# Attention by transposes of the bare exponentials: the one over the sums multiplies the values' sums instead of the probabilities

## The chip, the cores and the metric

The kernel runs on one NeuronCore of a Trainium2 chip. The metric is the device time of one execution in microseconds (us). Engines are named as in the profile: PE is TensorE's matmul side and PEld its weight load, DVE is VectorE, ACT is ScalarE, POOL is GpSimd, SP is SyncE.

## The reference

A model of 256 tokens of width 1024 runs through one hybrid block (a dilated attention of three groups of eight heads beside a state-space branch, then a gated feed-forward), and then, beside 256 context tokens, through four more layers: gated linear attention, a convolution, a full attention, gated linear attention again, each with a feed-forward. Everything is fp32. The change touches only the two softmax attentions:

```python
# hybrid block: 8 heads x 3 dilation groups, 256 queries, width 64 per head
logits = q @ k.T * HEAD_DIM ** -0.5 + bias          # causal, masked
p = exp(logits - m); o = (p @ v) / sum(p)           # for each group, then
attn = sum over the 3 groups of alpha * o           # alpha = softmax of the groups' log sums
# layer 2 of the second model: 16 query heads, 4 key heads, 512 tokens (256 + 256 context)
o = softmax(q @ k.T * ATTN_SCALE) @ v               # context queries see only the context's keys
```

The alpha-weighted sum over groups is the same as one softmax over the keys of all three groups, and the kernel computes it so: one maximum and one sum per head and query.

## The kernel before

The residual x lies in SBUF with features on the partitions. The weights stream in as 282 blocks of 1 MB through four raw buffers (SP issues the loads); ACT rounds each block to its high half (`split`, L1099), DVE makes the low half (L1716), and PE multiplies by three products, high-high, high-low and low-high (`three`, L493 to L498). No engine is scheduled by a planner: each engine's program is written out in order, and semaphores that count up join them. What stands in front of a waiting instruction on its engine goes first, always.

**The first attention** (hybrid block) runs beside eight blocks of the z projection. `PAIRS` (L376) are eight steps n: head pair j of 0 to 3, query tile qt of 0 and 1. A step has 6 key tiles of 128 when qt is 0 (3 groups, 2 heads, 1 tile) and 12 when qt is 1.
- PE, for each n (main loop of `products`): the scores of step n + 1 (L651), 3 parts of the z projection, the values of step n - 1 (`values`, L667), 2 parts, `turn(n)` (L672 to L683), 3 parts. A part is 6 matmuls of 256 columns. `turn` makes groups of up to four 128x128 tiles in banks 0 and 1 in turns; the third group of a qt = 1 step waits until DVE has taken the first. A turned tile is a matmul of the probabilities' tile (stationary) by a diagonal matrix that holds one over the sum of each query.
- ACT, for each n: the split of a z block, two exponentials with their sums (L1205), a copy of a z column, then after `recip_ready` two diagonals, identity times one over the sum (L1212), another z copy.
- DVE, for each n: after the exponentials the reciprocal (L1864), `front(n + 1)` (scores plus bias, maxima, L1842 to L1852), the split of a z block, the copies of the turned groups to SBUF (L1875), and after every second step `pair` (L1857), which copies 128x256 of values for the output projection. ACT and POOL then make its halves.
- After the loop PE goes on with four blocks of the output projection of this branch. They wait for a counter that DVE raises behind the last `pair` (L1885).

**The second attention** (layer 2) has nothing beside it. `PAIR_STEPS` (L446) are 32 steps n: head pair j of 0 to 7, query tiles in the order 0, 2, 1, 3. Tiles 0 and 1 see 512 keys, 2 and 3 see 256, so even n are wide (4 key tiles for each of the 2 heads) and odd n narrow (2 for each).
- PE, for each n: scores of n + 2 (L1001, after the exponentials of n have left its banks), `turn(n)` (L1013; by diagonals, one bank for each head), `values(n - 1)` (L1026; the two heads in the two column halves of the array). Turned banks 4 and 5, value banks 2 and 3.
- ACT, for each n: two exponentials with sums (L1541), then after the reciprocal two diagonals (L1550).
- DVE, for each n: maxima of n + 1 (L2392, L2396), copies of the turned tiles of n - 1 (L2409, one for each head), the reciprocal (L2402), and every fourth step a copy of 128x512 of values (`pair`, L2415).
- Four blocks of the output projection follow on PE (L496 to L498).

Of the kernel before, what the change touches and what calls it, by code (L numbers as in the profile page):

```python
# [132 lines left out]
class Role:  # L133
# [41 lines left out]
    "diag_ready", "head_squares", "heads_summed", "qstat_read", "qn_ready", "rot_ready", "rot_taken"])  # L175
# [111 lines left out]
def place(nc, ctx):  # L287
# [75 lines left out]
    with ExitStack() as st:  # L363
# [5 lines left out]
        b.diag = [[sb(st, f"diag{i}{j}", [P, P]) for j in range(2)] for i in range(2)]  # L369
# [16 lines left out]
def diagonal_of(b, n, odd):  # L386
    o = P * (2 * (n % 2) + odd)
    return b.sg[0][:, o:o + P]
# [58 lines left out]
SCORE_BANKS, TURNED_BANKS, VALUE_BANKS = ((0, 1), (6, 7)), (4, 5), (2, 3)  # L447

# [35 lines left out]
def products(nc, b, R, pe, ring):  # L484
# [187 lines left out]
    def turn(n):  # L672

        j, qt = PAIRS[n]
        for group in turned_groups(qt):
# [3 lines left out]
            for i, (odd, gr, kt) in enumerate(group):  # L679
                pe.wait_ge(R.sems["diag_ready"], 2 * n + odd + 1)  # L680
                last = mm(bank[m % 2][:, i * P:(i + 1) * P], b.logits[n % 2][:, odd, gr, kt * P:(kt + 1) * P],
                          diagonal_of(b, n, odd), start=True, stop=True)
            last.then_inc(*R.made("turned_ready"))  # L683

# [3 lines left out]
    for n in range(len(PAIRS)):  # L688
# [3 lines left out]
        if n:  # L692
            values(n - 1)
        go_on(parts, 2)
# [3 lines left out]
    values(len(PAIRS) - 1)  # L698
    R.next("turned_taken", R.value("m turned_ready"))
    R.next("diag_ready", 2 * len(PAIRS))  # L700
# [267 lines left out]
    def attention():  # L968
# [36 lines left out]
        def turn(n):  # L1005

            tiles = 4 if PAIR_STEPS[n][1] < 2 else 2
            for odd in range(2):
                pe.wait_ge(*R.next("diag_ready"))
                if n:  # L1010
                    pe.wait_ge(*R.next("turned_taken"))
                for i in range(tiles):
                    last = mm(bank[TURNED_BANKS[odd]][:, i * P:(i + 1) * P],  # L1013
                              b.prob[n % 2][odd][:, i * P:(i + 1) * P], b.diag[n % 2][odd][:], start=True, stop=True)
                last.then_inc(*R.made("turned_ready"))

        def values(n):
            j, qt = PAIR_STEPS[n]
            tiles = range(4) if qt < 2 else range(2, 4)
            pe.wait_ge(R.sems["turned_taken"], turned_before + 2 * (n + 1))  # L1020
            if n % 4 == 0 and j >= 2:
                pe.wait_ge(R.sems["part_lo"], parts_before + j - 1)
            for i, kt in enumerate(tiles):
                for odd in range(2):
                    base = HD * odd
                    last = mm(bank[VALUE_BANKS[j % 2]][base:base + HD, qt * P:(qt + 1) * P],  # L1026
                              b.av[:, kt, (j // 2) * HD:(j // 2 + 1) * HD], b.pt[n % 2][odd][:, i, :],
# [15 lines left out]
        R.next("exp_ready", 2 * GROUP_HEADS)  # L1043
# [6 lines left out]
        R.next("turned_taken", 2)  # L1050
        R.next("exp_ready", 4)
# [29 lines left out]
def splits_and_functions(nc, b, R, act, ring):  # L1081
# [114 lines left out]

    tables()
# [487 lines left out]
def vectors(nc, b, R, dve, ring):  # L1685
# [175 lines left out]
    for n, (j, qt) in enumerate(PAIRS):  # L1861
# [7 lines left out]
        if n:  # L1869
            dve.wait_ge(R.sems["values_ready"], 2 * n)  # L1870
# [752 lines left out]
```

## Time and profile before

| | us |
|---|---|
| three runs | 3223.01, 3230.93, 3230.63 (median 3230.63) |
| the profiled execution | 3230.28 |
| its span | 3228.5 |
| PE busy in it | 3042.9 (94%) |
| DVE, ACT, POOL busy | 1579.1 (49%), 1234.1 (38%), 302.0 (9%) |
| first attention, about | from 157 to 245 of the span |
| second attention, about | from 2220 to 2328 of the span |

The profile is one execution, taken by the hardware profiler. Lines are those of the kernel before. In a timeline the columns are the start in us from the span's start, the time in us, engine, line, operation, what it writes and reads, the shape, the number of instructions merged into the row, and in brackets the idle time before it and what ended it. An fp32 matmul is issued as two MATMUL records, a transpose as one. Ends of matmuls are modelled, so that one row overlaps the next: distances between starts are the better measure.

### The profile page before, as it was taken

The page shows a single profiled execution, that of the slowest core. Times are in us where ns is not written, and L with a number is a line of the kernel's source. Part 1 is how long each engine was busy: PE and PEld are TensorE (multiplying, and loading weights), DVE is VectorE, ACT ScalarE, POOL GpSimd, SP SyncE. Part 2 cuts the span into 40 slices and gives each one's busy share as a digit, 9 for nine tenths or more (in the row PEclk, how much of TensorE's full clock was granted, in tenths as well). Part 3 has the DMA queues.
Part 4 walks back from the last instruction along what each step waited for, and adds up shares of the span by engine and source line. Part 5 has one row for each costly group of instructions (what it writes and reads, how often), then busy time and mean ns, then how long its engine had stood idle before and what let it go on. Part 6 is the DMA issues. An engine that isn't in the chain of part 4 may idle for free.

```text
span 3228.5 us, 45698 instructions
## 1 busy us (share of the span) xinstructions
PE 3042.9 (94%) x19734; PEld 2493.5 (77%) x19734; DVE 1579.1 (49%) x2204; ACT 1234.1 (38%) x1756; POOL 302.0 (9%) x288
## 2 busy tenths in 40 slices
PE   8999888997998999999989999999999999897999
PEld 7898878996864778886657788876777888684799
DVE  4467756554456433333864333346643333446554
ACT  3245564445234422224344222344542223425443
POOL 1000001101001101111001001200010111000111
PEclk9999999998999999999999999999999999998899
DMA  7836314454210444224115432240044322221253
GB/s 281 305 114 233 131 53 170 165 180 179 93 52 27 158 168 152 97 92 144 66 40 192 162 130 93 103 148 27 14 169 170 138 97 92 80 79 37 108 183 131
DMA packets 59609, 407.66 MB, mean 126 GB/s; under 512 B 6504, under 2 KB 9832, under 8 KB 11024
## 3 DMA queue, kind: packets, MB, share of 16 engines
q1 hardware_dynamic: 58368, 401.02, 34.6%
q0 software_dynamic: 1040, 3.71, 0.4%
q8 instruction: 156, 2.56, 0.3%
q14 instruction: 45, 0.37, 0.0%
HBM read 403.62 MB, written 1.09 MB: 125 GB/s over the span
## 4 chain that ended last, share of the span: by engine, by line
PE 85%; DVE 7%; ACT 6%; issue 2%; POOL 1%; DMA 0%; DVEq 0%; ACTq 0%; POOLq 0%
PE bank L496 24%; PE bank L497 23%; PE bank L498 23%; PE bank L563 3%; DVE wlo L1716 2%; ACT whi L1099 2%; PE bank L932 1%; PE bank L572 1%; ACT part L1359 1%; PE bank L884 1%; PE bank L878 1%; PE bank L1013 1%; PE bank L888 1%; DVE small L2392 1%; ACT xnhi L1362 1%
## 5 line engine op out<-in xcount | busy, mean ns | idle before, releaser
L1716 DVE TENSOR_TENSOR wlo<-raw,whi 128x2048 fp32r<-128x2048 f32 x282 | 646.3, 2292 | 434.6 <-ACT whi L1099 434.2
L1099 ACT CAST whi<-raw 128x2048 fp32r<-128x2048 f32 x282 | 536.6, 1903 | 586.3 <-PE bank L498 586.2
L496 PE MATMUL bank<-xnhi,whi 128*128 128x512 f32 (+1 forms) x1776 | 681.5, 384 | 39.0 <-DVE xnlo L2101 14.3
L497 PE MATMUL bank<-xnlo,whi 128*128 128x512 f32 (+1 forms) x1776 | 664.6, 374 | 0.0
L498 PE MATMUL bank<-xnhi,wlo 128*128 128x512 f32 (+1 forms) x1776 | 662.4, 373 | 0.0
L496 PEld LDWEIGHTS bank<-xnhi,whi 128*128 128x128 f32 x1776 | 344.2, 194 | 140.7 <-issue 46.4
L498 PEld LDWEIGHTS bank<-xnhi,wlo 128*128 128x128 f32 x1776 | 344.7, 194 | 58.0
L497 PEld LDWEIGHTS bank<-xnlo,whi 128*128 128x128 f32 x1776 | 345.4, 194 | 53.0 <-issue 0.2
L496 PE MATMUL bank<-hidhi,whi 128*128 128x512 f32 (+1 forms) x1024 | 373.4, 365 | 0.2 <-DVE wlo L1716 0.2
L497 PE MATMUL bank<-hidlo,whi 128*128 128x512 f32 (+1 forms) x1024 | 371.6, 363 | 0.0
L498 PE MATMUL bank<-hidhi,wlo 128*128 128x512 f32 (+1 forms) x1024 | 371.3, 363 | 0.0
L496 PE MATMUL bank<-xn1hi,whi 128*128 128x256 f32 x992 | 295.8, 298 | 11.7 <-POOL xn1lo L1605 8.9
L497 PE MATMUL bank<-xn1lo,whi 128*128 128x256 f32 x992 | 285.0, 287 | 0.0
L498 PE MATMUL bank<-xn1hi,wlo 128*128 128x256 f32 x992 | 284.7, 287 | 0.0
L2120 DVE SCALAR_TENSOR_TENSOR x<-bank,mod,x 128x256 f32<-128x256 f32 x264 | 117.1, 479 | 328.5 <-PE bank L498 328.5
L1605 POOL TENSOR_TENSOR hidlo<-part,hidhi 128x512 fp32r<-128x512 f32 (+1 forms) x128 | 145.5, 1157 | 1079.4 <-ACT hidhi L1109 1079.4
L1587 ACT ACTIVATE sg<-bank 128x512 f32<-128x512 f32 (+1 forms) x128 | 69.6, 544 | 395.0 <-PE bank L498 395.0
L496 PEld LDWEIGHTS bank<-hidhi,whi 128*128 128x128 f32 x1024 | 193.2, 189 | 35.1 <-issue 4.9
L2452 DVE SCALAR_TENSOR_TENSOR part<-bank,sg 128x512 f32<-128x512 f32 (+1 forms) x128 | 79.9, 624 | 283.2 <-ACT sg L1587 262.2
L498 PEld LDWEIGHTS bank<-hidhi,wlo 128*128 128x128 f32 x1024 | 193.3, 189 | 30.3
L497 PEld LDWEIGHTS bank<-hidlo,whi 128*128 128x128 f32 x1024 | 193.3, 189 | 29.5
L496 PEld LDWEIGHTS bank<-xn1hi,whi 128*128 128x128 f32 x992 | 194.3, 196 | 26.6 <-issue 13.9
(317 smaller groups left out, 4301.7 us busy)
## 6 DMA issues: line engine op xcount, KB each, us to landing
raw<-in_wall SPq DMA_DIRECT2D x378, 1024.0 KB, 4.8
x<-in_x SPq DMA_DIRECT2D x2, 1024.0 KB, 7.3
bias<-relative_offsets POOLq DMA_DIRECT2D x2, 768.0 KB, 7.0
x<-relative_offsets POOLq DMA_DIRECT2D x2, 768.0 KB, 9.4
out<-x SPq DMA_DIRECT2D x1, 1024.0 KB, 4.8
vec<-in_vec SPq DMA_DIRECT2D x1, 665.0 KB, 9.7
cst<-in_cst SPq DMA_DIRECT2D x1, 465.0 KB, 10.3
rope<-in_rope POOLq DMA_DIRECT2D x1, 320.0 KB, 3.4
```

Source lines behind the costliest of these rows:

```text
L496: mm(out, wh, xh, start=first, stop=False)
L497: mm(out, wh, xl, start=False, stop=False)
L498: return mm(out, wl, xh, start=False, stop=last)
L563: last = mm(bank_of_sums[strip:strip + 32, 0:UC], b.cond[:, kk, :], w[:, kk, :], start=(kk < 4), stop=(kk >= 4))
L572: last = mm(bank_of_sums[:, o:o + 2], b.modrow[:, c * P:(c + 1) * P], cst("strips"), start=True, stop=True)
L878: last = mm(out[d], b.att[h % 2][d][half[d]:half[d] + 64, n[d] // 2, :], vv[d], start=(s % 4 == 0), stop=False)
L1099: nc.scalar.copy(b.whi[u % SPL][:], b.raw[pos % RAW][:]).then_inc(*R.made("hi_ready"))
L1587: fn(b.sg[c][:, 0:t], bank_of(c)[:, 0:t], ACT.Relu).then_inc(*R.made("gate_ready"))
L1605: tt(lo, src, hi, ALU.subtract).then_inc(*R.made("part_lo"))
L1716: ttn(b.wlo[u % SPL][:], b.raw[blocks[u] % RAW][:], b.whi[u % SPL][:], ALU.subtract).then_inc(*R.made("lo_ready"))
L2120: last = stt(b.x[:, ch, o:o + S], bank_of(c)[:, o:o + S], mcol(i, v, ch, s), b.x[:, ch, o:o + S], ALU.mult, ALU.add)
L2452: stt(part(t), bank_of(c)[:, 0:t], 0.0, b.sg[c][:, 0:t], ALU.max, ALU.mult) \
```

## The change

Both attentions turn the bare exponentials, by PE's transpose instead of a matmul by a diagonal. ACT makes no diagonals. One over the sums is made once for each head pair (second attention) or still each step but later in DVE's order (first), and PE spreads it in rows: `spread_inverses` multiplies each column of inverses, repeated 64 times as the stationary operand, by the identity, into a free half bank (first attention, 4 matmuls for each head pair) or bank 5 (second, 8 matmuls for each head pair). ACT copies that to SBUF (`copy_normaliser`), and `pair` on DVE multiplies the values' sums by it where it copied them. In the second attention the narrow steps turn both heads into one bank, so that DVE takes them with one copy of 512 columns instead of two of 256. New waits: transposes wait for the exponentials alone; ACT's exponentials of n wait until n - 2 is turned. The list of semaphores and the buffers `diag` change to match.

```diff
@@ -383,9 +382,15 @@
-def diagonal_of(b, n, odd):
-    o = P * (2 * (n % 2) + odd)
-    return b.sg[0][:, o:o + P]
+def inverses_of(b, j, first, tiles):
+    o = first + 2 * tiles * (j % 2)
+    return b.small[:, o:o + 2 * tiles].rearrange("p (q o) -> p q o", o=2)
+def turns_of_first():
+    return sum(len(turned_groups(qt)) for _, qt in PAIRS)
@@ -445,6 +450,25 @@
 SCORE_BANKS, TURNED_BANKS, VALUE_BANKS = ((0, 1), (6, 7)), (4, 5), (2, 3)
+def turns_by(n):
+    return 3 * ((n + 1) // 2) + 2 * ((n + 1) % 2)
+def turned_exps(b, n, odd):
+    return b.pt[0][odd][:, :, :] if n % 2 == 0 else b.pt[1][0][:, 2 * odd:2 * odd + 2, :]
+def normaliser_of(b):
+    return b.pt[1][1][:].rearrange("p a t -> p (a t)")
+def sums_of(b, j):
+    o = 48 * (j % 2)
+    return b.small[:, o:o + 8].rearrange("p (q o) -> p q o", o=2)
@@ -677,10 +701,22 @@
             for i, (odd, gr, kt) in enumerate(group):
-                pe.wait_ge(R.sems["diag_ready"], 2 * n + odd + 1)
-                last = mm(bank[m % 2][:, i * P:(i + 1) * P], b.logits[n % 2][:, odd, gr, kt * P:(kt + 1) * P],
-                          diagonal_of(b, n, odd), start=True, stop=True)
+                pe.wait_ge(R.sems["exp_ready"], 2 * n + odd + 1)
+                last = nc.tensor.transpose(bank[m % 2][:, i * P:(i + 1) * P],
+                                           b.logits[n % 2][:, odd, gr, kt * P:(kt + 1) * P], ident)
             last.then_inc(*R.made("turned_ready"))
+    def spread_inverses(out, inverses):
+        for qt in range(inverses.shape[1]):
+            for odd in range(2):
+                last = mm(out[odd * HD:(odd + 1) * HD, qt * P:(qt + 1) * P],
+                          inverses[:, qt, odd:odd + 1].to_broadcast([P, HD]), ident, start=True, stop=True)
+        last.then_inc(*R.made("norm_ready"))
+    def normaliser(j):
+        pe.wait_ge(R.sems["recip_ready"], 2 * j + 2)
+        spread_inverses(bank[5][:, S:T2], inverses_of(b, j, 32, 2))
@@ -691,13 +727,16 @@
             values(n - 1)
+            if n % 2 == 0:
+                normaliser(n // 2 - 1)
         go_on(parts, 2)
...
     values(len(PAIRS) - 1)
+    normaliser(GROUP_HEADS // 2 - 1)
     R.next("turned_taken", R.value("m turned_ready"))
-    R.next("diag_ready", 2 * len(PAIRS))
+    R.next("recip_ready", len(PAIRS))
     stage(4, b.ao, S, kc=4, fresh=True)
@@ -1005,26 +1044,35 @@
         def turn(n):
             tiles = 4 if PAIR_STEPS[n][1] < 2 else 2
+            if n:
+                pe.wait_ge(R.sems["turned_taken"], turned_before + turns_by(n - 1) - (tiles == 2))
             for odd in range(2):
-                pe.wait_ge(*R.next("diag_ready"))
-                if n:
-                    pe.wait_ge(*R.next("turned_taken"))
+                pe.wait_ge(R.sems["exp_ready"], exps_before + 2 * n + odd + 1)
+                if odd and n and n % 4 == 0:
+                    pe.wait_ge(R.sems["norm_copied"], norms_before + n // 4)
+                out = bank[TURNED_BANKS[odd if tiles == 4 else 0]]
+                o = odd * S if tiles == 2 else 0
                 for i in range(tiles):
-                    last = mm(bank[TURNED_BANKS[odd]][:, i * P:(i + 1) * P],
-                              b.prob[n % 2][odd][:, i * P:(i + 1) * P], b.diag[n % 2][odd][:], start=True, stop=True)
-                last.then_inc(*R.made("turned_ready"))
+                    last = nc.tensor.transpose(out[:, o + i * P:o + (i + 1) * P],
+                                               b.prob[n % 2][odd][:, i * P:(i + 1) * P], ident)
+                if odd or tiles == 4:
+                    last.then_inc(*R.made("turned_ready"))
+        def normaliser(j):
+            pe.wait_ge(R.sems["recip_ready"], recips_before + j + 1)
+            spread_inverses(bank[TURNED_BANKS[1]], inverses_of(b, j, 32, 4))
         def values(n):
...
             tiles = range(4) if qt < 2 else range(2, 4)
-            pe.wait_ge(R.sems["turned_taken"], turned_before + 2 * (n + 1))
+            pe.wait_ge(R.sems["turned_taken"], turned_before + turns_by(n))
             if n % 4 == 0 and j >= 2:
...
                     last = mm(bank[VALUE_BANKS[j % 2]][base:base + HD, qt * P:(qt + 1) * P],
-                              b.av[:, kt, (j // 2) * HD:(j // 2 + 1) * HD], b.pt[n % 2][odd][:, i, :],
+                              b.av[:, kt, (j // 2) * HD:(j // 2 + 1) * HD], turned_exps(b, n, odd)[:, i, :],
                               start=(i == 0), stop=(i == len(tiles) - 1))
@@ -1040,15 +1088,16 @@
         turned_before, parts_before = R.value("w turned_taken"), R.value("w part_lo")
-        R.next("exp_ready", 2 * GROUP_HEADS)
+        recips_before, norms_before = R.value("w recip_ready"), GROUP_HEADS // 2
+        exps_before = R.next("exp_ready", 2 * GROUP_HEADS)[1]
         for n in range(len(PAIR_STEPS)):
...
                 values(n - 1)
-        R.next("turned_taken", 2)
-        R.next("exp_ready", 4)
+            if n % 4 == 3:
+                normaliser(n // 4)
         values(len(PAIR_STEPS) - 1)
@@ -1194,6 +1243,10 @@
+    def copy_normaliser():
+        act.wait_ge(*R.next("norm_ready"))
+        nc.scalar.copy(b.sg[0][:, 0:S], bank[5][:, S:T2]).then_inc(*R.made("norm_copied"))
     tables()
@@ -1202,19 +1255,17 @@
             L = b.logits[n % 2][:, odd, :, 0:nk]
-            fn(L, L, ACT.Exp, bias=b.small[:, 20 + col:21 + col], accum_out=b.small[:, 24 + col:25 + col]) \
+            fn(L, L, ACT.Exp, bias=b.small[:, 20 + col:21 + col],
+               accum_out=b.small[:, 24 + col:25 + col]) \
                 .then_inc(*R.made("exp_ready"))
         z_column(0)
-        act.wait_ge(*R.next("recip_ready"))
-        o = CST["ident"][0]
-        for odd in range(2):
-            col = 28 + 2 * (n % 2) + odd
-            fn(diagonal_of(b, n, odd), b.cst[:, o:o + P], ACT.Copy, scale=b.small[:, col:col + 1]) \
-                .then_inc(*R.made("diag_ready"))
+        if n and qt == 0:
+            copy_normaliser()
         z_column(1)
...
             part(b.ao[0][:, n // 2 - 1, :], width=S)
+    copy_normaliser()
     part(b.ao[0][:, 3, :], width=S)
@@ -1534,21 +1585,20 @@
         def exponent(n):
-            nk = T2 if PAIR_STEPS[n][1] < 2 else S
+            j, qt = PAIR_STEPS[n]
+            nk = T2 if qt < 2 else S
             act.wait_ge(*R.next("neg_max"))
+            if n >= 2:
+                act.wait_ge(R.sems["turned_ready"], turns_of_first() + turns_by(n - 2))
             for odd in range(2):
...
                    bias=b.small[:, 20 + col:21 + col], scale=HD ** -0.5,
-                   accum_out=b.small[:, 24 + col:25 + col]).then_inc(*R.made("exp_ready"))
-        def diagonal(n):
-            act.wait_ge(*R.next("recip_ready"))
-            o = CST["ident"][0]
-            for odd in range(2):
-                col = 28 + 2 * (n % 2) + odd
-                fn(b.diag[n % 2][odd][:], b.cst[:, o:o + P], ACT.Copy, scale=b.small[:, col:col + 1]) \
-                    .then_inc(*R.made("diag_ready"))
+                   accum_out=sums_of(b, j)[:, qt, odd:odd + 1]).then_inc(*R.made("exp_ready"))
+        def copy_normaliser():
+            act.wait_ge(*R.next("norm_ready"))
+            nc.scalar.copy(normaliser_of(b), bank[TURNED_BANKS[1]][:]).then_inc(*R.made("norm_copied"))
@@ -1556,9 +1606,11 @@
             exponent(n)
-            diagonal(n)
+            if n and n % 4 == 0:
+                copy_normaliser()
             if n >= 5 and n % 4 == 1:
                 part(b.xn[0][:, n // 4 - 1, :], width=T2)
+        copy_normaliser()
         part(b.xn[0][:, KC - 1, :], width=T2)
@@ -1853,19 +1905,22 @@
     def pair(c):
         dve.wait_ge(R.sems["values_ready"], 4 * (c + 1))
-        cp(part(S).rearrange("p (a t) -> p a t", t=P),
-           bank[5][:, 0:S].rearrange("p (a t) -> p a t", t=P)[:, :, ::-1]).then_inc(*R.made("part_ready"))
+        dve.wait_ge(*R.next("norm_copied"))
+        way = lambda a: a.rearrange("p (a t) -> p a t", t=P)[:, :, ::-1]
+        ttn(part(S).rearrange("p (a t) -> p a t", t=P), way(bank[5][:, 0:S]), way(b.sg[0][:, 0:S]), ALU.mult) \
+            .then_inc(*R.made("part_ready"))
...
         col = 2 * (n % 2)
-        dve.wait_ge(*R.next("exp_ready", 2))
-        nc.vector.reciprocal(b.small[:, 28 + col:30 + col], b.small[:, 24 + col:26 + col]) \
-            .then_inc(*R.made("recip_ready"))
         if n + 1 < len(PAIRS):
...
         split()
+        dve.wait_ge(*R.next("exp_ready", 2))
+        nc.vector.reciprocal(inverses_of(b, j, 32, 2)[:, qt, :], b.small[:, 24 + col:26 + col]) \
+            .then_inc(*R.made("recip_ready"))
         if n:
@@ -2396,23 +2451,21 @@
-        def inverse(n):
-            col = 2 * (n % 2)
-            dve.wait_ge(*R.next("exp_ready", 2))
-            nc.vector.reciprocal(b.small[:, 28 + col:30 + col], b.small[:, 24 + col:26 + col]) \
-                .then_inc(*R.made("recip_ready"))
+        def inverse(j):
+            dve.wait_ge(*R.next("exp_ready", 8))
+            nc.vector.reciprocal(inverses_of(b, j, 32, 4), sums_of(b, j)).then_inc(*R.made("recip_ready"))
         def take_turned(n):
             nt = 4 if PAIR_STEPS[n][1] < 2 else 2
-            for odd in range(2):
+            for odd in range(2 if nt == 4 else 1):
                 dve.wait_ge(*R.next("turned_ready"))
-                cp(b.pt[n % 2][odd][:, 0:nt, :],
-                   bank[TURNED_BANKS[odd]][:, 0:nt * P].rearrange("p (a t) -> p a t", t=P)) \
+                cp(b.pt[n % 2][odd][:, :, :], bank[TURNED_BANKS[odd]][:].rearrange("p (a t) -> p a t", t=P)) \
                     .then_inc(*R.made("turned_taken"))
         def pair(j):
             dve.wait_ge(*R.next("values_ready", 4))
-            cp(part(T2), bank[VALUE_BANKS[j % 2]][:]).then_inc(*R.made("part_ready"))
+            dve.wait_ge(*R.next("norm_copied"))
+            ttn(part(T2), bank[VALUE_BANKS[j % 2]][:], normaliser_of(b), ALU.mult).then_inc(*R.made("part_ready"))
@@ -2422,13 +2475,12 @@
         for n in range(len(PAIR_STEPS)):
-            if n == 0:
-                inverse(0)
             if n + 1 < len(PAIR_STEPS):
...
                 take_turned(n - 1)
-                inverse(n)
+            if n % 4 == 3:
+                inverse(n // 4)
             if n >= 5 and n % 4 == 1:
```

## Rows read from the trace of the kernel before

**Rows 1.** The page, part 4: the chain that ended last, by engine.
```profile
PE 85%; DVE 7%; ACT 6%; issue 2%; POOL 1%; DMA 0%; DVEq 0%; ACTq 0%; POOLq 0%
```

**Rows 2.** Windows: length, busy us by engine, granted clock, DMA share, GB/s; the two attentions.
```profile
160.00:250.00 90.00, 85.67 (x768) 79.15 (x768) 56.62 (x88) 39.75 (x77) 4.60 (x6) 1.00 0.34 112
2232.00:2320.00 88.00, 86.43 (x750) 62.81 (x750) 63.74 (x169) 51.50 (x166) 7.65 (x6) 1.00 0.01 1
```

**Rows 3.** Timeline of PE, one round of two steps in the second attention.
```profile
2235.89 1.13 PE L1001 MATMUL bank<-aqk 64*128 64x512 f32 x4
2236.95 2.05 PE L1013 MATMUL bank<-diag,prob 128*128 128x128 f32 x16
2238.93 0.66 PE L1026 MATMUL bank<-pt,av 128*64 128x128 f32 x8
2239.51 0.70 PE L1001 MATMUL bank<-aqk 64*128 64x256 f32 x4
2240.33 1.16 PE L1013 MATMUL bank<-diag,prob 128*128 128x128 f32 x8
2241.42 1.09 PE L1026 MATMUL bank<-pt,av 128*64 128x128 f32 x16
2242.48 1.13 PE L1001 MATMUL bank<-aqk 64*128 64x512 f32 x4
```

**Rows 4.** Timeline of DVE and ACT in that round.
```profile
2237.09 1.29 DVE L2392 TENSOR_REDUCE small<-bank 128x1 f32<-128x512 f32 x2 [1.54 <-PE bank L1001]
2238.49 1.28 DVE L2409 COPY pt<-bank 128x512 f32<-128x512 f32 x2
2239.76 0.67 DVE L2415 COPY part<-bank 128x512 f32<-128x512 f32 x1
2240.35 0.74 DVE L2392 TENSOR_REDUCE small<-bank 128x1 f32<-128x256 f32 x2
...
2240.99 0.68 ACT L1541 ACTIVATE prob<-bank,small 128x512 f32<-128x512 f32 x1
```

**Rows 5.** Groups of PE by line and shape: records, busy us, mean ns.
```profile
L1013 PE MATMUL bank<-diag,prob 128*128 128x128 f32 x384 | 52.4, 287 | 3.5 <-ACT diag L1550 2.0
L713 PE MATMUL bank<-cst,xs 128*128 128x128 f32 x32 | 4.8, 276 | 2.8 <-DVE dt L1926 1.6 <-DVE xdt L1940 1.1
```

**Rows 6.** Timeline of PE: four transposes in the linear attention, and what follows.
```profile
881.36 0.60 PE L827 MATMUL bank<-cst,part 128*128 128x128 f32 x4
881.88 0.69 PE L832 MATMUL bank<-qb,part 128*64 128x64 f32 x16
```

**Rows 7.** Timeline of PE in the first attention: turned tiles and what follows them.
```profile
165.10 1.50 PE L681 MATMUL bank<-sg,logits 128*128 128x128 f32 x12
...
175.76 3.07 PE L681 MATMUL bank<-sg,logits 128*128 128x128 f32 x24
178.59 0.36 PE L496 MATMUL bank<-xn1hi,whi 128*128 128x256 f32 x1
...
221.44 1.16 PE L681 MATMUL bank<-sg,logits 128*128 128x128 f32 x8 [0.81 <-DVE turned L1875]
```

**Rows 8.** Timeline at the end of the first attention.
```profile
243.45 1.53 PE L667 MATMUL bank<-turned,v 128*64 128x128 f32 x24
245.05 0.42 DVE L1857 COPY part<-bank 128x256 f32<-128x256 f32 x1 [1.66 <-PE bank L667]
...
245.63 0.36 PE L496 MATMUL bank<-aohi,whi 128*128 128x256 f32 x1 [0.66 <-issue]
```

**Rows 9.** Timeline of PE: first and last wide step turned in the second attention.
```profile
2222.86 3.07 PE L1013 MATMUL bank<-diag,prob 128*128 128x128 f32 x16
...
2322.04 2.05 PE L1013 MATMUL bank<-diag,prob 128*128 128x128 f32 x16 [0.60 <-ACT diag L1550]
```

**Rows 10.** Windows, columns as in rows 2: linear attention's end; modulation rows before it.
```profile
1031.00:1040.00 9.00, 9.00 (x62) 3.79 (x60) 6.79 (x16) 2.48 (x8) 2.50 (x2) 1.00 0.00 0
788.00:798.00 10.00, 8.37 (x61) 4.34 (x60) 5.16 (x10) 5.97 (x12) 0.00 (x0) 0.50 0.85 308
```

More of the change, by code:

```diff
@@ L174 @@
     "dw_based", "dw_ready", "mean_summed", "mean_ready", "mean_taken", "centred", "ln_ready",
-    "diag_ready", "head_squares", "heads_summed", "qstat_read", "qn_ready", "rot_ready", "rot_taken"])
+    "norm_ready", "norm_copied", "head_squares", "heads_summed", "qstat_read", "qn_ready", "rot_ready", "rot_taken"])
 def unit_plan():
@@ L368, in place @@
         b.pt = [[sb(st, f"pt{i}{j}", [P, 4, P]) for j in range(2)] for i in range(2)]
-        b.diag = [[sb(st, f"diag{i}{j}", [P, P]) for j in range(2)] for i in range(2)]
     b.bank = [ctx.enter_context(nc.psum_tensor(f"bank{i}", [P, 512], F32)) for i in range(8)]
```

## The prediction

> **What bounds the kernel now.** The chain that ended last comes first: PE holds 85% of it and no DMA is in it [rows 1], so a stage shortens only if PE's own time or PE's waits in it shrink. Then the windows of the two attentions [rows 2]. In both PE is busy nearly throughout (85.7 of 90 us and 86.4 of 88 us) at the full granted clock; DVE has 72% of the second, ACT 59%, the DMA engines almost nothing. So both attentions are PE's, and the reader should see that the two engines that lose work here, ACT and a little of DVE, are not what bounds.
>
> The timeline of one round of the second attention (a wide step and a narrow one) says what PE does with its time [rows 3]. From start to start: wide scores 1.06, wide turning 1.98, narrow values 0.58, narrow scores 0.82, narrow turning 1.09, wide values 1.06; the next round begins 6.59 us after this one. Turning is 3.07 of it, 47%. The narrow scores themselves need about 0.62 (0.70 busy less an overlap of 0.08, as elsewhere in these rows), so 0.20 a round is a wait, for a diagonal. The first round is slower, and the last wide turning waited 0.60 for its diagonal [rows 9].
>
> **The change, part by part.**
>
> *Turning.* An fp32 matmul leaves two records, a transpose one: 192 matmuls of the second attention are 384 records, the 32 transposes of the state-space part are 32 [rows 5]. Eight records more cost 1.98 - 1.09 = 0.89, 0.111 each [rows 3]. Four transposes took 0.52 to the next line's start, 0.11 or so each plus a remainder [rows 6]. So one 128x128 tile falls from 0.22 to 0.11. The bounds of the price: 0.11 below, and 0.15 above, the 4.8 us over 32 of the state-space part [rows 5], which holds the tails of short bursts; I take the lower with a remainder of 0.12 a burst. Wide turning becomes 1.00 (between 8 x 0.11 + 0.08 and the 1.09 of eight matmul records), narrow 0.56 (0.52 to 0.64). That saves 0.98 + 0.53 = 1.51 a round.
>
> *Normaliser on PE, second attention.* Eight matmuls for each head pair, 64 columns wide, the two heads in alternate halves of the array: the shape of the wide values, sixteen records, 1.06 [rows 3]. It could be no less; at worst 2 x 1.06 if stationary operands that are one column repeated load slowly. I take 1.06, or 0.53 a round. The inverse that it waits for is made on DVE right behind the copy that the values before it wait for, so it should find it ready.
>
> *A round afterwards.* 1.06 + 1.00 + 0.58 + 0.62 + 0.56 + 1.06 + 0.53 = 5.41. Now what is late next. DVE finished the maxima and began the first copy 2.60 after the round's start and the second 0.64 later [rows 4]; it still does so, for the maxima depend on the scores alone. The narrow turning would start at 3.26 (1.06 + 1.00 + 0.58 + 0.62) and needs the first copy, at 3.24 and a handing-over of 0.06; the wide values would start at 3.85 and need the second, at 3.94. That is 0.1 of wait. So 5.5 a round against 6.57 (13.15 for four steps), and 1.07 saved. DVE's own sum: 1.40 maxima, 1.20 copies, 0.85 narrow maxima [rows 4], 0.64 for one 512-column copy instead of two of 256, half of a pair's 0.6, that is 4.4 to 4.7 of 5.5: it fits, with little to spare. ACT loses 1.4 of diagonals a round and gets a copy of 512 columns each second one, about as long as an exponential's 0.68 [rows 4]. That copy stands behind the exponentials of step 4k and ahead of those of 4k + 1, and waits for PE's normaliser, whose results are there some 0.2 us into the round of step 4k. Copy to 0.9, two narrow exponentials at 0.5 to 0.7 each to 2.3 at the latest; the narrow scores that need their banks start at 2.64: covered by at least 0.3. Without the cover each microsecond late costs one, eight times. The wait on the turning of n - 2 lies a round back and is met. `pair` as a product reads one operand more; I cost it like the copy, 0.67 [rows 4], and up to twice that, which would make DVE late in four-step turns by at most 0.6 x 8.
>
> *Second attention, sum.* Fifteen ordinary rounds 16.0. In the first round the wide turning took 3.07 at a clock that was mostly half, against 2.05 later [rows 9]; with half the records 1.5 goes, and 0.4 of waits. In the last, the 0.60 for the diagonal goes. Together 18.5. The last normaliser stands ahead of the last values, so the `pair` behind them is not later; the output projection reaches its last eighth some 5 us after it starts anyway.
>
> *First attention.* PE has z parts to do between, but it is the bound all the same, so less turning is time. Turning 12 tiles took 2.83 to the next line [rows 7]; 6 tiles half of that less a wait, 1.3. Two of the four turnings of 12 had to wait longer for DVE (0.81 in one [rows 7]); about 18 us in all for eight steps. Afterwards 6 x 0.11 = 0.66, and for 12 tiles the third group must wait for the first to be copied: 0.60 (four transposes to their end [rows 6]), 0.06, a copy of 0.69, 0.06, then 0.44: 1.85. Four of each: 10.0, if DVE is on time. It should be: the reciprocal moves behind `front(n + 1)` and the split on DVE, so these two no longer wait for the exponentials, and nothing on PE but the normaliser waits for the reciprocal. This saves 7.9. Three normalisers in the loop, 8 records like narrow values, 0.58 each, take 1.7. The fourth stands in an open chain: values end, DVE copies at 245.05, PE goes on at 245.63 [rows 8]; now a normaliser 0.58, ACT's copy (0.4, at most 0.68) and handings lie between, 1.1. Net 5.1. No DMA is issued elsewhere; SP's loads are released by the splits and by nothing else here.
>
> *Total.* 23.6 off the profiled execution's 3230.3, which lies 0.4 under the median: **3206.7**, so 3207. The runs before lie 8 apart; a difference under 0.3% (10 us) is what a measurement of this kernel can't tell from none.
>
> **A rule that speaks against it.** In the linear attention's end PE did nothing but matmuls on a half or a quarter of the array and a few transposes, and the granted clock was 1.00 for 9 us; in the modulation rows, PE busy 8.4 of 10 us with matmuls 32 columns wide, it was 0.50 throughout [rows 10]. [...] After the change only half-array matmuls and transposes are left in the second attention, the full-array matmuls are gone. The Trainium skill, page "TensorE: Matmul & The Clock Gate", section "Part 4: PE-mode transpose", says that transposes don't count as busy for the clock and the full rate does not engage for them; by this page alone the stage would lean on the scores, values and normalisers, and might run at half clock, 3241 to 3275 by the sums of the third rival below instead of 3207. No row here shows a stretch of transposes alone.
>
> **The rivals.**
> 1. *Forecast*, chance 0.75: 3207.
> 2. *DVE's copies are late*, 0.13: with one set of turned banks, PE waits in every round for a copy, by one copy's length (0.64). For it: DVE at 80% of the round and a margin of 0.0 to 0.1. Against it: DVE starts the maxima as soon as the scores are there. 16 x 0.64 = 10: 3217. With both copies late, 3227, which is no change.
> 3. *The clock falls in the second attention*, 0.06, slower. PE's 5.41 a round becomes 5.41 x 1.8 = 9.7 (the factor between the 1.5 of the first, partly slow turning [rows 9] and the 2 of the two levels, nearer to 2 because that turning ended at full clock). All the stage: +3.1 x 16 = +50, 3275 with the 5 of the first attention off. Half of the time, which I take as the case: +16 x (7.6 - 6.57) = +16, less 5 in the first attention, 3241. It decides from about a third of the stage. Against it: the 9 us at 1.00 of half-array work [rows 10].
> 4. *A transpose costs as much as the matmul here*, 0.02: only waits go (3.2 + 0.6 + some 1), and normalisers stay (8.5 + 1.7 + 1.1): 3230 + 6.5 = 3237. The single records of rows 5 and 6 speak against it.
> The rest, 0.04, is a small gain under 10 us from several of these.
>
> **How the numbers follow.** The forecast's own range: the tile's price (0.11 to 0.13 over 264 tiles, +5), the runs' spread of 8 and 2 of clock phases elsewhere: 3199 to 3212. With the second rival the range is 3199 to 3217. Slower by over 0.3%: 0.08 (3 and 4); within 0.3%: 0.07 (the worse end of 2, and the rest); faster: 0.85.
>
> **What would show it.** In the profile after: turned tiles as 192 and 72 single records at distances of 0.11; rounds of 5.5 in the second attention, no PE wait on ACT in them, waits on DVE's copies under 0.2 each; the wide values of a round 1.06; the stage from first scores to output projection 18 to 19 us shorter; clock 1.00 from the second round on. In the first attention the third group of each qt = 1 step waits about 0.5 for DVE, and the gap ahead of the output projection grows by 1. A stage at clock 0.5, rounds over 6, or ACT held by `norm_ready` past the scores of the next step would make it wrong.

## The result and the profile after

The kernel after takes 3210.48 us (median of four runs, 3206.19 to 3212.88), the kernel before beside it 3226.82 (four runs, 3222.85 to 3230.93). The ratio is 0.9946, 95% interval 0.9933 to 0.9959: 16.3 us or 0.5% faster. The forecast was 3207, with a range of 3199 to 3217. So the total fell into the range, but partly for wrong reasons. One of the two attentions gave 0.6 us more than forecast, and the other 7.8 us less.

The profiled execution took 3206.19 us with a span of 3204.4 (before 3228.5). The chain that ended last, by engine:

```profile
PE 86%; DVE 6%; ACT 5%; issue 1%; POOL 1%; DMA 0%; DVEq 0%; ACTq 0%; POOLq 0%
```

It is PE's as before [rows 1]. Each attention is measured from its first scores to the first matmul of its output projection. For the second attention of the kernel before, that is from 2208.02 to 2327.93 of the span, so it starts some 12 us before the "about 2220" given above:

| us | before | after | change | forecast |
|---|---|---|---|---|
| first attention | 88.27 | 82.58 | -5.7 | -5.1 |
| second attention | 119.90 | 109.24 | -10.7 | -18.5 |
| from the first attention's end to the second's start | 1962.39 | 1955.07 | -7.3 | 0 |
| whole span | 3228.5 | 3204.4 | -24.1 | -23.6 |

The two attentions together give 16.4, close to the 16.3 of the medians. The 7.3 between them lie in code that the change does not touch; the experiments show below that they come and go without it. The span's 24.1 against the forecast's 23.6 is therefore an accident.

Windows of the kernel after, with the columns of rows 2: the first attention, the start of the second, and its rest.

```profile
160.00:235.00 75.00, 72.59 (x662) 66.47 (x662) 52.50 (x82) 32.11 (x59) 3.13 (x4) 1.00 0.37 125
2204.00:2212.00 8.00, 6.11 (x23) 3.37 (x23) 5.73 (x14) 1.64 (x6) 0.00 (x0) 0.57 0.01 3
2212.00:2300.00 88.00, 78.01 (x754) 51.79 (x752) 63.21 (x145) 41.70 (x131) 8.76 (x7) 1.00 0.00 1
```

In the second attention PE is busy 78.0 of 88 us, where before it was 86.4 of 88 [rows 2]: a tenth of the stage has become idle. The granted clock is 1.00 throughout. So the clock does not explain the missing gain; PE waits. For what, the waits of PE in this stage say (in total, how often, the longest):

```profile
PE bank L1040 <- ACT prob L1595: 9.0, 6, 1.5
PE bank L1024 <- DVE aqk L2414: 3.8, 1, 3.8
PE bank L1040 <- DVE aqk L2422: 1.9, 1, 1.9
PE bank L1056 <- DVE pt L2462: 1.0, 1, 1.0
```

The first line is new: six times 1.5 us for ScalarE's exponentials. The two lines below it stand in the kernel before too, at its lines 985 and 1001. The last is one wait at the end of the stage, where the kernel before waited for diagonals. The timeline of PE over four steps shows the place:

```profile
2219.39 1.13 PE L1040 MATMUL bank<-aqk 64*128 64x512 f32 x4
2220.45 1.10 PE L1056 MATMUL bank<-cst,prob 128*128 128x128 f32 x8
...
2223.32 1.09 PE L1074 MATMUL bank<-pt,av 128*64 128x128 f32 x16
2225.92 1.13 PE L1040 MATMUL bank<-aqk 64*128 64x512 f32 x4 [1.50 <-ACT prob L1595]
2226.98 1.09 PE L1056 MATMUL bank<-cst,prob 128*128 128x128 f32 x8
2228.01 0.66 PE L1074 MATMUL bank<-pt,av 128*64 128x128 f32 x8
2228.59 0.70 PE L1040 MATMUL bank<-aqk 64*128 64x256 f32 x4
2229.26 0.66 PE L1056 MATMUL bank<-cst,prob 128*128 128x128 f32 x4
2229.86 1.09 PE L1074 MATMUL bank<-pt,av 128*64 128x128 f32 x16
2230.78 1.04 PE L713 MATMUL bank<-cst,small 128*64 128x128 f32 x16
2231.76 1.13 PE L1040 MATMUL bank<-aqk 64*128 64x512 f32 x4
```

The rounds alternate: 6.53 from 2219.39 to 2225.92 with the wait, 5.84 from there to 2231.76 without. Before, they took 6.56 and 6.59 in turns ([rows 3] show a 6.59). Turned tiles are single records as forecast: wide turning takes 1.03 to the next start, narrow 0.60, the normaliser 0.98. What ScalarE waited for stands in its timeline and DVE's in the late round:

```profile
2220.59 1.29 DVE L2447 TENSOR_REDUCE small<-bank 128x1 f32<-128x512 f32 x2 [1.63 <-PE bank L1040]
2221.91 0.17 DVE L2451 TENSOR_SCALAR small<-small 128x2 f32<-128x2 f32 x1
2221.99 1.28 DVE L2462 COPY pt<-bank 128x512 f32<-128x512 f32 x2
2223.19 0.68 DVE L2468 TENSOR_TENSOR part<-bank,pt 128x512 f32<-128x512 f32 x1
...
2223.90 0.62 ACT L1158 CAST xnhi<-part 128x512 fp32r<-128x512 f32 x1 [2.89 <-DVE part L2468]
2224.43 0.68 ACT L1595 ACTIVATE prob<-bank,small 128x512 f32<-128x512 f32 x1
```

The maxima of step 4k + 2 are known at 2222.08. Its exponentials start at 2224.43, 2.35 later, though ScalarE was idle for 2.89. Ahead of them in ScalarE's order stands a cast of the head pair's values (`part`, issued where n is 4k + 1). It waits for DVE's product, which stands behind the two copies. Everything in this chain (maxima, copies, product, cast, two exponentials, PE's scores that need their bank) was there before the change. PE simply used to be slower than it. From start to start, the rows give scores 1.20, maxima 1.40, copies 1.20, product 0.71, cast 0.53 and exponentials 1.49, which is 6.53 in all.

In the first attention the change did what was forecast. PE's timeline, a step with 12 tiles, and the end:

```profile
175.06 1.04 PE L705 MATMUL bank<-cst,logits 128*128 128x128 f32 x8
176.51 0.66 PE L705 MATMUL bank<-cst,logits 128*128 128x128 f32 x4 [0.41 <-DVE turned L1930]
176.92 0.36 PE L520 MATMUL bank<-xn1hi,whi 128*128 128x256 f32 x1
...
236.86 1.53 PE L691 MATMUL bank<-turned,v 128*64 128x128 f32 x24
238.22 0.61 PE L713 MATMUL bank<-cst,small 128*64 128x128 f32 x8
238.87 0.37 ACT L1248 COPY sg<-bank 128x256 f32<-128x256 f32 x1 [1.37 <-PE bank L713]
239.33 0.42 DVE L1912 TENSOR_TENSOR part<-bank,sg 128x256 f32<-128x256 f32 x1 [2.53 <-ACT sg L1248]
...
239.92 0.36 PE L520 MATMUL bank<-aohi,whi 128*128 128x256 f32 x1 [1.09 <-issue]
```

Twelve tiles take 1.86 to the next line (before 2.83 [rows 7]). From the last values to the output projection it is 3.06 instead of 2.18 [rows 8].

### The profile page after: what moved, and what is told of

The parts are those of the page before. It is cut to its first block, busy times and chain, and to the rows that moved or that the text cites. A ratio compares the mean times of both kernels' runs of the same rounds, so it can differ in the third digit from the quotient of the medians.

```text
span 3204.4 us, 45388 instructions
## 1 busy us (share of the span) xinstructions
PE 3015.1 (94%) x19630; PEld 2464.6 (77%) x19630; DVE 1573.4 (49%) x2164; ACT 1215.1 (38%) x1688; POOL 301.8 (9%) x288
## 3 DMA queue, kind: packets, MB, share of 16 engines
HBM read 403.62 MB, written 1.09 MB: 126 GB/s over the span
## 4 chain that ended last, share of the span: by engine, by line
PE 86%; DVE 6%; ACT 5%; issue 1%; POOL 1%; DMA 0%; DVEq 0%; ACTq 0%; POOLq 0%
PE bank L520 25%; PE bank L521 24%; PE bank L522 23%; PE bank L587 3%; DVE wlo L1768 2%; ACT whi L1148 1%; PE bank L596 1%; PE bank L971 1%; PE bank L923 1%; ACT part L1410 1%; PE bank L917 1%; PE bank L1040 1%; PE bank L927 1%; PE bank L1056 0%; ACT xnhi L1413 0%
```

## The experiments

Eight kernels were run, four of them more than once (experiments 1, 2, 4 and 5); the other times are single executions. "Two steps" and "four steps" are distances between the starts of scores in the first and the second attention; "stage" is as in the table above. The kernel before ran on the same chips (medians 3224.08 and 3224.12).

**1. The cast later.** The suspected wait alone is taken out of its place; the work stays.

```diff
@@ ScalarE, loop over the second attention's steps n
-            if n >= 5 and n % 4 == 1:
+            if n >= 6 and n % 4 == 2:
                 part(b.xn[0][:, n // 4 - 1, :], width=T2)
```

> The changed kernel with one edit: in the second attention ACT rounds the pair's values (the cast that waits for the multiplication by the normaliser) behind the exponentials of step 4k + 2 instead of ahead of them. In the changed kernel PE waits 1.50 us for ACT once in four steps, and four steps take 12.37. Theory A (the cast waits for DVE's pair and holds the exponentials of 4k + 2, whose maxima are ready 2.3 us earlier): the wait goes, four steps take 10.9 to 11.0, the stage from its first scores to the output projection 99 to 101 us instead of 109.3, and the kernel is about 9 us faster than the changed one, near 0.992 of the one before. Rival B (DVE's order, copies and pair ahead of the maxima, is what is late): the wait stays at 1.0 or more, four steps over 12, no more than 2 us gained.

Measured: 3197.72 us (3196.89 to 3198.67), ratio to before 0.9916 (0.9901 to 0.993). Its interval lies wholly under that of the kernel after. The stage is 100.22, 9.0 shorter, which is the six waits of 1.50. Four steps are 4.96 + 5.84 = 10.80. DVE and ACT around the cast, and the window of the stage:

```profile
2224.58 0.17 DVE L2451 TENSOR_SCALAR small<-small 128x2 f32<-128x2 f32 x1
2224.65 1.28 DVE L2462 COPY pt<-bank 128x512 f32<-128x512 f32 x2
2224.78 0.69 ACT L1595 ACTIVATE prob<-bank,small 128x512 f32<-128x512 f32 x1 [1.10 <-DVE small L2451]
2225.85 0.68 DVE L2468 TENSOR_TENSOR part<-bank,pt 128x512 f32<-128x512 f32 x1
...
2226.57 0.62 ACT L1158 CAST xnhi<-part 128x512 fp32r<-128x512 f32 x1 [0.34 <-DVE part L2468]
```
```profile
2212.00:2295.00 83.00, 82.04 (x782) 55.08 (x780) 67.12 (x152) 45.22 (x137) 8.88 (x7) 0.99 0.01 1
```

The exponentials now start with their maxima's end, and what ends ScalarE's idle time is DVE's small tile, not `part`. PE is busy 82.0 of 83 us. That settles the cause of the missing time, and this kernel beats both others.

**2. The product ahead of the copies.** It shortens the same chain at another link and leaves the cast where it was.

```diff
@@ DVE, loop over the second attention's steps n
+            if n >= 5 and n % 4 == 1:
+                pair(n // 4 - 1)
             if n:
                 take_turned(n - 1)
             if n % 4 == 3:
                 inverse(n // 4)
-            if n >= 5 and n % 4 == 1:
-                pair(n // 4 - 1)
```

> The kernel after with one move on VectorE: the product of the head pair is issued ahead of the two copies of the turned exponentials of step 4k+1's round, not behind them. ScalarE's cast stays between the exponentials of 4k+1 and 4k+2. Theory A (ScalarE's queue is held at that cast until the product lands): the cast can start about 1.28 us earlier (the two copies that stood ahead of the product), so the exponentials of 4k+2 are no longer late by 1.5 us but by 0.2 or so; in exchange the copies stand 0.68 later, and TensorE's values of 4k wait some 0.3 to 0.7 for them. Four steps come to 11.2 to 11.7 us, the stage to 102 to 106 us, the kernel 4 to 7 us under the kernel after. Theory B (VectorE's whole work in that round is too long and ScalarE's order does not matter): the same work stands in the round, so four steps stay at 12.4 and the stage at 109.

Measured: 3201.45 us (3199.41 to 3201.81), ratio 0.9923 (0.9906 to 0.9939). Four steps are 5.75 + 5.83 = 11.58, the stage 104.64. The waits of PE in the stage:

```profile
PE bank L1056 <- DVE pt L2462: 5.7, 8, 0.8
PE bank L1024 <- DVE aqk L2414: 3.8, 1, 3.8
```

The wait for the exponentials is gone, though DVE's work is the same, so theory B falls. In its place PE waits up to 0.8 for the copies, which now stand behind the product. This is the second rival of the prediction, made real: DVE's order has no room for 0.68 us ahead of the copies.

The kernel gained more than the 4 to 7 us that were expected: 9.0 from median to median, or 6.3 if each is taken against the kernel before in its own comparison (22.7 against 16.3). The stage explains 4.6 of it; the rest was not traced.

**3. The cast later in the kernel before.**

> The kernel before with the cast of the pair's values moved on ScalarE behind the exponentials of 4k+2, as in the first experiment. Theory A (the wait exists only because the change made TensorE's round shorter than the chain product, cast, exponentials): in the kernel before the chain was covered, so the second attention stays at 119 to 120 us, four steps at 13.1. Theory B (the cast's place costs the same in both kernels and the change only inherits it): the stage shortens by 6 to 9 us here too, to 111 to 113.

Measured: the stage 118.59 (before 119.90), rounds 6.55 and 6.56, one run of 3222.70. Theory A. Before the change the queue cost at most 0.03 a round. It became a cost only as PE's own round fell under 6.53.

**4. and 5. One attention at a time.** The first of these kernels has the change in the first attention alone, the other in the second alone.

> Only the first attention changed, the second as before. Theory: by the two traces the first attention's end came 5.7 us earlier, so this one is 5 to 7 us faster than the kernel before (ratio about 0.998), with two steps in 20.05 us instead of 22.06. Rival (the other 7 us that the changed kernel's trace gains between 300 and 800 us belong to the change, not to the phase of the clock): 10 to 13 us faster.

> Only the second attention changed, the first as before. Theory: its stage takes 109.3 us as in the changed kernel instead of 119.9, the kernel is 10 to 11 us faster than before (ratio about 0.9967), the gains of the two halves add up. Rival (part of the gain of the second attention needs the first's): stage above 111 us.

Measured: first alone 3217.85 us (3216.26 to 3227.18), ratio 0.9982 (0.9972 to 0.9992); second alone 3213.09 us (3211.18 to 3219.77), ratio 0.9971 (0.9961 to 0.9982). Two steps of the first are 20.03 where it is changed, 21.70 to 22.07 where not (the later ones; the earliest pairs are shorter in both). The second's stage is 109.24 where it is changed, 119.33 where not. The gains of 6.2 and 11.0 us add up to 17.2, against 16.3 for both. So the rival of 10 to 13 us for the first alone falls, and no effect of one part on the other is visible beyond the spread of the runs. The trace of the first attention alone has a stage of 84.12 and that of the second alone, whose first attention is the old one, 89.15. Both began at a lower granted clock (0.79 from 157 to 165), and there the gain is 5.0; at full clock from the start it is the 5.7 of the table.

**6. Matmuls by the identity instead of transposes.** The new order of the work stays, the cheaper operation goes.

```diff
@@ both turnings (that of the second attention is shown)
-                    last = nc.tensor.transpose(out[:, o + i * P:o + (i + 1) * P],
-                                               b.prob[n % 2][odd][:, i * P:(i + 1) * P], ident)
+                    last = mm(out[:, o + i * P:o + (i + 1) * P],
+                              b.prob[n % 2][odd][:, i * P:(i + 1) * P], ident, start=True, stop=True)
```

> The changed kernel with fp32 matmuls by the identity instead of transposes, in both attentions; all else as changed. Theory (a transpose is worth half of a matmul's 0.22 us): the wide turning takes 1.98 instead of 1.02 again and the narrow 1.09 instead of 0.6. In the half of four steps in which PE waits 1.5 us for ACT the 1.5 us more are absorbed, in the other half they show: four steps about 13.9, the stage about 121, so the change without transposes is no gain in the second attention (13.15 before). First attention: two steps 22 us or more. Rival (the gain came from waits for diagonals that went, not from the transposes): four steps under 13.

Measured: one run, 3236.28. The stage is 122.34, four steps 6.53 + 7.25 = 13.78. PE's timeline in the free half:

```profile
2242.74 2.05 PE L1056 MATMUL bank<-cst,prob 128*128 128x128 f32 x16
2244.72 0.66 PE L1074 MATMUL bank<-pt,av 128*64 128x128 f32 x8
2245.31 0.70 PE L1040 MATMUL bank<-aqk 64*128 64x256 f32 x4
2245.94 1.16 PE L1056 MATMUL bank<-cst,prob 128*128 128x128 f32 x8
2247.03 1.09 PE L1074 MATMUL bank<-pt,av 128*64 128x128 f32 x16
```

Wide turning is 1.98 to the next start again, narrow 1.09. The free half grew by 7.25 - 5.84 = 1.41, close to the 0.95 + 0.49 = 1.44 by which these rows differ from those of the kernel after. The other half did not grow at all: there 1.4 us more of matmuls took the place of 1.5 of waiting. In the first attention two steps take 21.66, less than the 22 expected, and the stage 90.03. That stage began at a granted clock of 0.79, so it has to be compared with others that did: 89.15 with the old first attention (experiment 5) and 84.15 with the new one (experiment 1). The whole gain of the change is thus the transposes' price. Without it the reordering and the normaliser cost 2.4 us in the second attention and 0.9 in the first.

**7. The normaliser twice** (second attention, the eight matmuls issued a second time into the same bank).

> The kernel after with the eight matmuls that spread a head pair's inverses issued twice, to the same bank (second attention alone). Their records last 0.98 to 1.04 us for a pair. Theory A (they lie on TensorE's path, in the half of the four steps that ScalarE does not hold up): four steps 12.37 plus about 1.0 = 13.4, the stage 109.2 plus 7 to 8 = 116 to 117.5. Rival (the wait for the exponentials absorbs them): four steps stay within 0.3 of 12.37.

Measured: four steps 6.53 + 6.71 = 13.24, the stage 116.76, 7.5 more than after. The waits for ScalarE are still 9.0 in all. A normaliser costs 6.71 - 5.84 = 0.87 where it stands. It stands in the half that nothing covers.

**8. The reciprocal early** (first attention).

```diff
@@ DVE, loop over the first attention's steps n
+        dve.wait_ge(*R.next("exp_ready", 2))
+        nc.vector.reciprocal(...).then_inc(*R.made("recip_ready"))
         if n + 1 < len(PAIRS):
             front(n + 1)
         split()
-        dve.wait_ge(*R.next("exp_ready", 2))
-        nc.vector.reciprocal(...).then_inc(*R.made("recip_ready"))
```

> The kernel after with the first attention's reciprocal of the sums put back on VectorE to the place where the kernel before had it, ahead of the maxima of the next step; it waits for the exponentials there. Theory A (TensorE is the bound, VectorE has slack in the first attention): what VectorE does late, the third group of turned tiles, comes 0.3 to 0.6 us later in each step or so, two steps last 20.2 to 21.2 instead of 20.0, the stage 83 to 87 instead of 82.6. Rival (the reciprocal's place is free): two steps stay at 20.0 and the stage at 82.6 to 82.8.

Measured: two steps 20.16 at first, then 20.97 and 21.32, the stage 86.53, one run of 3214.77. That is 3.9 more than the 82.58 of the kernel after, but not all of it is the reciprocal's. This execution began the stage at a lower granted clock than the kernel after, whose same window stands at 1.00:

```profile
157.00:165.00 8.00, 8.00 (x57) 7.04 (x57) 4.76 (x11) 1.68 (x5) 0.25 (x1) 0.79 0.27 115
```

Experiments 1 and 2 leave the first attention as it is in the kernel after, and began it at 0.79 too: their stage is 84.15 in both. Against them the early reciprocal costs 2.4. The wait of PE for turned tiles (the kernel after, then this one):

```profile
PE bank L705 <- DVE turned L1930: 1.7, 4, 0.4
```
```profile
PE bank L705 <- DVE turned L1930: 3.8, 4, 1.6
```

These waits hold 2.1 of the 2.4. The move of the reciprocal behind the maxima and the split, which looks like a detail of the change, is worth 2.4 of the 5.0 us that the first attention gains in executions that start so (89.15 less 84.15).

**The 7 us between the attentions.** The ten profiled executions show how long the untouched code from the first attention's output projection to the second's first scores took:

| kernel | us | kernel | us |
|---|---|---|---|
| before | 1962.39 | second alone | 1954.33 |
| after | 1955.07 | matmuls by the identity | 1960.31 |
| cast later | 1955.42 | normaliser twice | 1961.28 |
| product ahead | 1955.95 | reciprocal early | 1959.69 |
| first alone | 1955.49 | before, cast later | 1954.39 |

There are two clusters, 1954 to 1956 and 1959.7 to 1962.4. The kernel before with its cast moved, which has nothing of the change, is among the short ones, and three variants that have the whole order of the change are among the long ones. So the 7.3 in the first table are not the change's. Part of it can be seen: the kernel before falls 4.2 us behind "before, cast later", which has the same code here, between 399 and 475 of the span. The window 400 to 450 of the two, the kernel before first:

```profile
400.00:450.00 50.00, 43.74 (x365) 39.97 (x364) 25.65 (x47) 29.14 (x69) 0.00 (x0) 0.90 0.20 75
```
```profile
400.00:450.00 50.00, 43.72 (x402) 39.74 (x402) 28.56 (x55) 33.63 (x76) 0.00 (x0) 1.00 0.21 72
```

The granted clock of this window is 0.90 to 0.93 in the four long executions and 1.00 in the six short ones.

## Why the prediction was right, and where it was not

*What bounds.* Right. Both attentions are PE's, and both shortened when PE's work did.

*Turning.* Right. Wide 1.03 and narrow 0.60 against 1.00 and 0.56, and single records. Experiment 6 takes the difference away again.

*Normaliser.* Estimated at 1.06 a head pair, which "could be no less". It was less: 0.98 by its row, 0.87 to 0.88 by what it adds to a round (5.84 against 4.96 in experiment 1, experiment 7).

*A round afterwards.* PE's sum of 5.41 was right: (4.96 + 5.84) / 2 = 5.40 in experiment 1. So was the claim that DVE's copies are just in time. The 0.1 of wait for them did not come, and experiment 2 shows how near it was. The step that failed is the next one, "what is late next". For ScalarE the prediction followed only the copy of the normaliser, found it "covered by at least 0.3", and expected no PE wait on ACT. The cast that stands between the exponentials of 4k + 1 and 4k + 2 was not in the account. Its product was priced only as DVE's time. What was missed is a floor, and it could have been read in the kernel before: the wide scores start at 2235.89 [rows 3], the next wide exponentials at 2240.99 [rows 4], 5.10 later. In the kernel after, the distance in the late round is 5.04, and the scores follow 1.49 behind. The same 1.49 added to the 5.10 gives 6.59, the very round of the kernel before. Every kernel that kept the chain whole has this half at 6.53 (after, second alone, matmuls by the identity, normaliser twice, reciprocal early), whatever PE had to do in it. The other half, with the normaliser and no cast, is PE's own.

*Second attention.* The forecast of 18.5 missed the 9.0 of waits and was otherwise 1.2 too low: 10.7 + 9.0 = 19.7, which is the 119.90 - 100.22 of experiment 1. The 0.1 a round forecast for DVE's copies, which did not come, is more than enough for those 1.2 (16 x 0.1).

*First attention.* 5.7 against 5.1. Twelve tiles took 1.86 (1.85 forecast), the third group waits 0.41 on the row. The open chain at the end grew by 0.9 instead of 1.1. The reciprocal's move was named as the condition for DVE being on time, and experiment 8 shows that it was one, worth 2.4.

*Rivals.* DVE's copies were not late. The clock did not fall: 1.00 from 2212 to 2300, with half-array matmuls and transposes alone. The Trainium skill, page "TensorE: Matmul & The Clock Gate", section "Part 4: PE-mode transpose", says that the full rate does not engage for transposes. This stage kept it with them, but does not show what transposes alone would do: turning takes 2 x (1.03 + 0.60) = 3.3 us of the 10.8 of four steps in experiment 1, and the rest is matmuls. A transpose did not cost as much as the matmul (1.03 against 1.98 for eight tiles).

*Its own signs.* The prediction named "rounds over 6" as what would make it wrong, and "no PE wait on ACT" as what would show it. Every second round was 6.53 with a wait of 1.50 on ACT, so by its own signs it was wrong for the second attention, whatever the total says.

*The numbers.* The gain was forecast at 23.6 and came to 16.3; the difference is the 7.8 missing in the second attention less the 0.6 more in the first. The time is still only 3.5 over the forecast of 3207, because the forecast was taken off 3230.3, and the median of the kernel before in the same comparison was 3226.8. The range held it, and that is partly luck: 16.3 off 3230.3 would have been 3214, beyond the forecast's own 3199 to 3212, and inside 3217 only by the price of the second rival, which did not come.

## What to carry to other kernels

When the bounding engine's part of a loop gets shorter, write out for every other engine its whole order in one round, each instruction with what it waits for, and compute the longest loop through them (here scores, maxima, copies, product, cast, exponentials, scores: 6.53). That is the new floor, however little of their time those engines are busy: ScalarE was idle for 2.89 us in front of the instruction that made everything late.

A cheap consumer that nobody needs soon does not belong ahead of a producer that somebody waits for. Moving one cast by one step gave 9.0 us; the transposes themselves give 19.0 in the two stages (122.34 - 109.24, and 90.03 - 84.15 between executions that began the first attention at the same clock).

Compare a stage only with one that had the same granted clock. Here the first attention took 82.58 or 84.15 with the same code, and a comparison across the two charges 1.6 us to whatever edit stands between them.

If one part of a forecast misses and the total still fits, compare stage by stage: the profiled difference of 24.1 against 23.6 would have hidden a miss of 8.

## What the runs showed that was not expected

- A stationary operand that is one column repeated 64 times loads like any other: 16 records in 0.98 to 1.04, with 137 ns for a weight load (PEld), the same as for the values' operands.
- The first turning of the second attention, eight transposes in a window with a granted clock of 0.57 (2204 to 2212), took 1.90 to the next start; the same eight at 1.00 take 1.03:

```profile
2209.31 1.97 PE L1056 MATMUL bank<-cst,prob 128*128 128x128 f32 x8
2211.21 0.80 PE L1040 MATMUL bank<-aqk 64*128 64x256 f32 x4
```

- Stretches at a lower granted clock in untouched code make executions of any of these kernels differ by some 6 to 7 us. The first scores of the first attention show it in small: the same code took a stage of 84.15 with the window 157 to 165 at 0.79 (experiment 1) and 82.58 with it at 1.00 (the kernel after), with rounds of 20.01 in both. Windows of experiment 1, then of the kernel after:

```profile
157.00:165.00 8.00, 7.58 (x53) 6.51 (x53) 4.19 (x10) 1.41 (x5) 0.00 (x0) 0.79 0.36 131
```
```profile
157.00:165.00 8.00, 7.66 (x66) 7.02 (x67) 5.83 (x12) 1.68 (x5) 0.83 (x1) 1.00 0.32 127
```

What starts such a stretch at one time and not at another stays open.
